# Two blocks of a transformer on one core: the order of turns, gate products and splits at the feed-forwards' first units and at the mLSTM's end

## What is computed

```python
def sublayer(x, fn, g_pre, g_post, shift, scale, gate, weight):
    hmod = rms_norm(x, g_pre) * (1 + scale[:, None, :]) + shift[:, None, :]
    y = rms_norm(fn(hmod), g_post)
    return x + weight * gate[:, None, :] * y
def swiglu(h, w1, w3, w2):
    return (jax.nn.silu(h @ w1) * (h @ w3)) @ w2
```

## Time and profile before

| | us |
|---|---|
| runs of the kernel | 1457.6, 1462.0, 1462.41 |
| median | 1462.0 |
| profiled execution: its time | 1460.16 |
| its span in the profile | 1458.4 |
| PE busy | 97% of the span |
| DVE busy | 69% |
| ACT busy | 49% |
| mean granted clock of PE | 0.993 |

### The profile page before, as it was taken

The page is one execution under the profiler, slowest core; times in us unless marked ns, Lnnn a source line. Parts: engine busy times, 40 slices in busy tenths (PEclk is TensorE's granted clock), DMA queues, the critical chain, the costliest instruction groups (busy, mean ns, idle before and its releaser), DMA issues.

```text
span 1458.4 us, 18473 instructions
## 1 busy us (share of the span) xinstructions
PE 1418.3 (97%) x7578; PEld 1206.9 (83%) x7578; DVE 1012.4 (69%) x1239; ACT 718.3 (49%) x925; POOL 91.6 (6%) x112
## 2 busy tenths in 40 slices
PE   9899999998999999999999999999999999999998
PEld 8788887886888877888879978778888799999886
DVE  5877666986977668777768965678755544553765
ACT  5443347456443454434565676454434644554433
POOL 1000001002000010000100352010000100000000
PEclk9999999999999999999999999999999999999999
DMA  9888855854987738888535411578764455445543
GB/s 386 343 318 302 315 200 215 314 180 173 385 313 307 287 131 346 310 321 324 184 145 188 162 70 69 176 294 333 296 211 150 176 209 179 133 157 190 187 153 120
DMA packets 51396, 337.41 MB, mean 231 GB/s; under 512 B 6720, under 2 KB 9584, under 8 KB 11376
## 3 DMA queue, kind: packets, MB, share of 16 engines
q1 hardware_dynamic: 51312, 336.23, 61.6%
HBM read 335.12 MB, written 1.09 MB: 231 GB/s over the span
## 4 chain that ended last, share of the span: by engine, by line
PE 78%; DVE 8%; ACT 5%; DMA 4%; issue 2%; POOL 2%; SPq 0%; DVEq 0%; POOLq 0%; ACTq 0%
PE ps L952 75%; DMA raw<-units 4%; DVE wlo L1584 3%; ACT whi L486 2%; PE ps L1171 1%; DVE M L1588 1%; POOL base L407 1%; DVE x L1677 1%; DVE hf L1971 1%; ACT hf L560 1%; ACT M L551 1%; POOL ssx L408 1%; PE ps L1062 1%; ACT M L543 0%; PE ps L1432 0%
## 5 line engine op out<-in xcount | busy, mean ns | idle before, releaser
L1584 DVE TENSOR_TENSOR wlo<-raw,whi 128x2048 fp32r<-128x2048 f32 x228 | 522.4, 2293 | 221.3 <-ACT whi L486 220.7
L952 PE MATMUL ps<-whi,xhi 128*128 128x512 f32 x1472 | 586.0, 398 | 12.7 <-DVE wlo L1584 8.4
L952 PE MATMUL ps<-whi,xlo 128*128 128x512 f32 x1472 | 575.9, 391 | 0.0
L952 PE MATMUL ps<-wlo,xhi 128*128 128x512 f32 x1472 | 575.3, 391 | 0.0
L486 ACT ACTIVATE whi<-raw 128x2048 fp32r<-128x2048 f32 x228 | 435.9, 1914 | 164.7 <-DMA raw<-units 164.5
L952 PEld LDWEIGHTS ps<-whi,xhi 128*128 128x128 f32 x1472 | 278.1, 189 | 76.8 <-DVE wlo L1584 12.1
L952 PEld LDWEIGHTS ps<-whi,xlo 128*128 128x128 f32 x1472 | 277.5, 189 | 59.8
L952 PEld LDWEIGHTS ps<-wlo,xhi 128*128 128x128 f32 x1472 | 278.0, 189 | 54.9 <-issue 0.2
L952 PE MATMUL ps<-xhi,whi 128*128 128x256 f32 x704 | 202.0, 287 | 0.0
L952 PE MATMUL ps<-xhi,wlo 128*128 128x256 f32 x704 | 199.2, 283 | 0.0
L952 PE MATMUL ps<-xlo,whi 128*128 128x256 f32 x704 | 199.2, 283 | 0.0
(11 more groups left out here) (226 smaller groups left out, 864.9 us busy)
## 6 DMA issues: line engine op xcount, KB each, us to landing
raw<-units SPq DMA_DIRECT2D x228, 1024.0 KB, 4.9
M<-ada_units SPq DMA_DIRECT2D x82, 1024.0 KB, 7.0
gp<-gate_rows SPq DMA_DIRECT2D x7, 512.0 KB, 7.7
M<-cvec SPq DMA_DIRECT2D x2, 512.0 KB, 4.3
x<-x_in SPq DMA_DIRECT2D x1, 1024.0 KB, 6.0
ada_a<-ada_units SPq DMA_DIRECT2D x1, 1024.0 KB, 18.7
ada_b<-ada_units SPq DMA_DIRECT2D x1, 1024.0 KB, 22.7
M<-bias_by_distance SPq DMA_DIRECT2D x2, 512.0 KB, 6.4
```

The source lines that it names most:

```text
L952: return pe.matmul(out, lhsT, rhs, start=start, stop=stop, skip_group_check=True)
L1584: dve.tensor_tensor(wlo[:, s, :], raw[:, s, :], whi[:, s, :].bitcast(F32), ALU.subtract)\
```

## The change

Four edits. In unit 2 of each feed-forward the turn of unit 1 stands behind the first of the two products of the second half, not ahead of it. On DVE, `gate_up(0, 1)` stands ahead of the split of unit u0 + 4 in stages 2, 3 and 5, and the gate products of unit 2 stand ahead of the split of its second weight unit. SiLU of the second c in stage 5 goes from the head of ACT's `first_two` to behind its second split. At the end of stage 1 the last ada product, `ada_done` and `mod_columns` stand between `new_x` and `normed_x`, and the split of u and `gate_columns` between `normed_x` and `modulated`.

```diff
--- before.py
+++ after.py
@@ -642,9 +642,7 @@
                         act.activation(xhi[:, 8 + 2 * (i % 4):10 + 2 * (i % 4), :], ps[:, 6, :], ACT.Copy)\
                            .then_inc(S["gt_hi"], 1)
 
-                    if n == 5:
-                        silu_c(1)
-                    first_two(n, silu)
+                    first_two(n, silu, (lambda: silu_c(1)) if n == 5 else None)
                     gated_hi(0)
                     for i in range(2, NF):
                         a = up_unit(n, i, 0)
@@ -1182,8 +1180,11 @@
                         by_token(a, 0, 0, 4)
                         pe.wait_ge(g_ok[i > 2], b + i)
                         by_token(a, 0, 1, 5).then_inc(w_used, 1)
-                        turn(i - 1)
+                        if i > 2:
+                            turn(i - 1)
                         by_token(a + 1, 1, 0, 4).then_inc(s1_ok, 1)
+                        if i == 2:
+                            turn(1)
                         by_token(a + 1, 1, 1, 5).then_inc(w_used, 1)
                         if n == 0 and i == 5:
                             pe.wait_ge(S["bias_in"], 48)
@@ -1684,7 +1685,14 @@
                     lo(u + 1)
                 gated_y(n, 0)
                 new_x(n, 0)
+                if late:
+                    ada(ADA_FIRST[n] + 9)
+                    ada_done(ADA_FIRST[n] + 9)
+                    mod_columns(n + 1)
                 normed_x(n + 1, 0)
+                if late:
+                    lo(u)
+                    gate_columns(n + 1)
                 modulated(n + 1, 2)
                 split_x(n + 1, 0, 0)
                 modulated(n + 1, 3)
@@ -1772,9 +1780,9 @@
 
                     gate_up(0, 0, 4)
                     gate_up(1, 0, 5)
+                    gate_up(0, 1, 6)
                     if n:
                         lo(u0 + 4)
-                    gate_up(0, 1, 6)
                     lo(u0 + 5)
                     if n == 5:
                         dve.wait_ge(S["c_ok"], 2)
@@ -1791,9 +1799,12 @@
                         if some:
                             ada(v)
                         gated_lo(i - 1)
-                        lo(a + 4)
+                        if i > 2:
+                            lo(a + 4)
                         gate_up(i, 0, 4)
                         gate_up(i, 1, 5)
+                        if i == 2:
+                            lo(a + 4)
                         lo(a + 5)
                         if some:
                             ada(v + 1)
@@ -1928,11 +1939,6 @@
                     lo(u0 + 15)
                     turned_lo(1, (1,))
                     ada(v + 8)
-                    ada(v + 9)
-                    lo(u0 + 16)
-                    ada_done(v + 9)
-                    mod_columns(2)
-                    gate_columns(2)
                     boundary(n, True)
                 if kind == "mb":
                     R = lambda j: dtt[0:H_MB, j, :]
```

## The result

| | before | changed |
|---|---|---|
| runs, us | 1457.6 to 1462.41 (4) | 1449.71 to 1452.32 (4) |
| median, us | 1461.44 | 1451.28 |
| profiled execution: its time | 1460.16 | 1449.71 |
| its span | 1458.4 | 1447.9 |
| its mean granted clock | 0.993 | 0.991 |

The changed kernel is faster. The ratio of the runs is 0.9947, 95% interval 0.9929 to 0.9965, which is 7.7 us (5.1 to 10.4) of 1462.0 and leads to 1454.3; the two medians lie 10.2 apart, the two profiled executions 10.45. Forecast were 11.9 us, 1448.2, with a range up to 1452.5. The direction and the places were right, the size came out short.

What follows compares the result with a forecast made beforehand. PE, busy 97% of the span, was taken as the bound, with gains only from its waits and half clock. From 1460.16 us, -2.72 - 2.72 - 1.54 - 1.77 - 1.28 - 1.9 = -11.9 gave 1448.2; range 1444.5 to 1452.5.

Steps and rivals of the forecast that it cites:

- The second turns: Unit 2 of n = 0 and n = 3: a product fills PE's wait ahead of the turn, -2.72 us each.
- First gate products: Start of n = 2 and 5: gate product ahead of DVE's split removes the first turn's wait, -1.77 and -1.28 us.
- Unit 3: PE, arriving earlier, finds unit 2's gate product ready; tightest spare 0.6 us in n = 5; costed at nothing.
- SiLU of c: n = 5: moved behind ACT's part of a split, into ACT's wait for PE; costed at nothing.
- Rival (b): Gains of n = 0, 2 and 5 are waited for again at unit 3: 1454.0 us, chance 0.07.
- The mLSTM's end: End of n = 1: normed x comes earlier, so PE turns it at its due time; -1.9 us.
- 0.5 as the limit: Sign of being wrong: GpSimd's root at the mLSTM's end ends less than 0.5 us ahead of PE's due time.
- Rival (c): mLSTM gain is nil: product 35 and small operations delay normed x past 333.13; 1450.1 us, chance 0.05.
- The clock: Behind the second turn of n = 0: shorter idle time means no fall to half clock, -1.54 us.
- rival (a): Clock falls elsewhere, at the mLSTM's end: 1449.7 us with one fall, 1451.3 with two; chance 0.14.
- Half clock shows up in new places: Sign of being wrong: the changed profile has PE at half clock where it was not before; no size given.
- Rival (d): Slower: the later turn hands its lateness on to unit 3 in four units; 1465.3 us, chance 0.02.

Runs made afterwards that it cites:

- experiment 3: Kernel before with only the first gate product ahead of the split and SiLU of c later: median 1457.44 us, ratio 1.0003.
- experiment 5: Kernel before with later second turn and first gate product ahead of the split, but without unit 2's new gate order or the mLSTM edit: 1451.37 us, ratio 0.9949.
- experiment 7: Changed kernel plus four small products of ones ahead of each of five late Mamba head pairs: 1444.71 us, ratio 0.9909 to the kernel before.
- experiment 2: Kernel before with only the later second turn and unit 2's gate products ahead of its split: 1453.31 us, ratio 0.9968.
- experiment 4: Kernel before with only the edits at the mLSTM's end: 1457.32 us, ratio 0.9989.
- experiment 11: Kernel before with 11 small products of ones in the second turn's wait of n = 0, no turn moved: 1456.82 us, ratio 0.9979.
- the pair with fillers: Changed kernel and kernel before, each with four small products of ones ahead of five Mamba head pairs: 1444.71 and 1458.11 us.
- experiment 6: Kernel before with all of the change's feed-forward edits, without those at the mLSTM's end: 1448.81 us, ratio 0.9931.
- fillers of 2: Changed kernel plus two small products of ones ahead of each of five late Mamba head pairs: 1445.26 us, ratio 0.9907 to the kernel before.

## Why the prediction was right or wrong

**The second turns: right.** In n = 0 the turn starts at 59.98 with 0.26 idle (forecast near 59.87, 0.4 or less) and a whole product more is done. In n = 3 it starts at 556.26 without a wait. The stage gave 3.39 where 2.72 was counted. In the kernels whose second turn of n = 3 is unchanged its idle time was 2.66, 1.67, 2.34, 2.14 and (experiment 3) 1.78, so this number differs between executions, and with it the gain. Why it does is not shown.

**First gate products: right.** n = 2 gave 2.02 and n = 5 1.52 against 1.77 and 1.28, and experiment 3 shows the dependence on the cover. **Unit 3: right.** No wait for a gate product appears in the changed kernel, and experiment 5 shows 1.54 us of it in three places without the new order. SiLU of c cost nothing visible. Rival (b), that the gains are waited for again at unit 3, falls.

**The mLSTM's end: right.** 2.10 against 1.9, and 2.1 between any profile with the edit and any without. GpSimd's operation on one column was held, as the prediction took it: 1.44 us from 323.95, to the end of product 35 (324.08 + 1.22), against 0.30 at 320.54, when none ran. The Trainium skill states on the page "SBUF — State Buffer", section "Who interferes with whom", that a VectorE instruction with two inputs in SBUF contends with a GpSimd instruction that reads SBUF; the trace now agrees for an ada product too. The modulation columns had to run anyway and covered most of it, so DVE waited only 0.27 us for the root; the root ended 2.2 us ahead of PE's turn (325.47 + 0.57 to 328.28), where I had set 0.5 as the limit. The three waits behind it are 3.07 us, less than my 4.5. Rival (c) falls.

**The clock: wrong, and this is the step that failed.** "With idle time down to about 0.4 us I expect no fall: -1.54" was true of this pair of profiles: no fall at 60. Its size was right as well, 1.7 us between profiles with and without the fall. As a term of the kernels' difference it was not sound, because it took the clock of one profiled execution as a property of the kernel. Two of four profiles with that gap show no fall. The prediction called n = 3 the nearest case, a longer idle time with no fall behind it; two of five profiles do have a fall there. Both places together, about half of one fall at each, come to some 1.5 us on the average (my estimate from four falls in nine such gaps at 1.7 us), so the sum was not far off for the mean of many executions; it was no forecast for four. And the range reached up only "past two more falls" of 1.54 each, placed by rival (a) at the mLSTM's end, where the changed kernel has none (336 to 340 us: 1.00). The falls that count sit in Mamba's last heads, in both kernels, from none to over 20 us of half clock in one execution. From the waiting product of Mamba to the turn of x behind it the profiles need 144.3 us (experiment 7, with fillers) to 151.8 (experiments 2, 4 and 11); before had 147.4, after 150.8. Experiment 3, with no half clock in the heads and no fillers, needs 144.6. That is up to 7.3 us between executions of the same Mamba instructions, more than the range's 4.3 above the forecast. "Half clock shows up in new places" was one of the prediction's own signs of being wrong, and it came true, though at 267 it costs nothing. The sum put the clock in Mamba at nothing and the range gave it no room: I had looked at PE's clock where the change touches the program, and at no window of the stage with the smallest products.

**Why 7.7 and not 11.9.** The four executions of the first comparison had a clock of 0.989, 0.989, 0.991 and 0.991, on the average 0.0034 under the 0.9934 of the kernel before: by the slope 3.3 us of bad luck. At an equal clock they are as far ahead as all others. Their mean, 1451.15, is 7.8 under 1458.9, the mean of the 80 executions of the kernel before, while the four of it in the table have a mean of 1460.7; that may be why the ratio gives less than the two medians there, but the record doesn't say. The later measurements gave 0.9933, 0.9932 and 0.9915, that is 9.8, 9.9 and 12.4 us. Whether the clock term holds on the average stays open: the means as they are, 10.2 apart, give about 1.4 us either way, which is nearer to 10.4 than to 11.9; the pair with fillers gives 12.2.

**Rival (d)**, slower by lateness handed on, showed nowhere.

## What to carry to other kernels

A wait of one product's length can be filled by moving a product ahead of the waiting step, and then what the engine now reaches earlier has to be moved as well: the first gate product alone was worth 1 us or nothing, with the later turn it was worth its 3.0 us (by the stretches of n = 2 and 5, experiment 6 against 2), and without unit 2's new order 2.0 us of it all were waited for again. Before a half clock is counted as a term, look at several executions. Comparing at an equal mean granted clock (a line through time against clock) halved the uncertainty of the difference here, from about 1.4 us either way to 0.7; and comparing single stretches between profiles told 2.1 us from nothing where a ratio (experiment 4) could not. Where PE ran small products for a long stretch, a few products of ones in it held the clock: with fillers of 2 the changed kernel came to 1445.3, with fillers of 4 to 1444.7, the best version tried (13.3 us under the kernel before by its ratio).

## What the runs showed of the hardware

- The same idle time, 2.98 or 2.99 us in the same place, was followed by half clock in two profiles and by full clock in two; behind shorter idle times of 2.14 and 2.34 us there was half clock, and behind one of 2.66 there was none.
- The same half clock costs 1.7 us in a stretch where PE sets the pace (170.7 against 169.0 in n = 0) and nothing where the splits do (31.86 to 31.89 us at the mLSTM's end, with it and without).
- The clock stayed at 1.2 GHz for 17 to 20 us in Mamba's last heads while PE was busy for 6.00 of 6.00 us; with 1.06 us of ones ahead of five of the pairs of heads, the same stretch ran at 2.4 GHz. A whole execution of the kernel before ranges from 1453.8 to 1465.2 us; at one mean granted clock the executions lie within about 1.5 us of their line (one standard deviation), where without it the standard deviation is 2.6.
